# Neighbourhood attention in tiles of 64 queries of two heads by 128 keys, on one Trainium2 core

## What is computed

```python
col_start = np.clip(c - WIN_COLS // 2, 0, GRID_W - WIN_COLS)
col_mask = (c[None, :] >= col_start[:, None]) & (c[None, :] < col_start[:, None] + WIN_COLS)
s = jnp.einsum("brwhd,brkvhd->bhrwkv", qg, k_rows,
               preferred_element_type=jnp.float32) * (NA_HEAD_DIM ** -0.5)
s = jnp.where(col_mask[:, None, :], s + bias, NEG_INF)
p = jax.nn.softmax(s.reshape(B, NA_HEADS, rows, GRID_W, kr * GRID_W), axis=-1)
o = jnp.einsum("bhrwkv,brkvhd->brwhd", p, v_rows)
```

## Time and profile before

| | us |
|---|---|
| median of three runs | 2140.15 |
| lowest, highest | 2139.81, 2140.32 |
| span of the profiled execution | 2138.8 |
| TensorE busy in it | 2126.1 (99%) |
| VectorE busy | 1417.7 (66%) |
| ScalarE busy | 1094.5 (51%) |

### The profile page before, as it was taken

One profiled execution on the slowest core, in us unless ns is written; L12 is line 12 of the kernel. 1 busy time (PEld: TensorE's weight loads), 2 busy tenths in 40 slices (PEclk: granted clock), 3 DMA queues, 4 the chain that ended last, 5 costly groups with the idle time before them and its releaser, 6 DMA issues.

```text
span 2138.8 us, 27241 instructions
## 1 busy us (share of the span) xinstructions
PE 2126.1 (99%) x9684; PEld 1758.9 (82%) x9684; DVE 1417.7 (66%) x1952; ACT 1094.5 (51%) x1515; POOL 59.7 (3%) x70
## 2 busy tenths in 40 slices
PE   9999999999999999999999999999999999999999
PEld 7888887888888888888877888888888888888887
DVE  6998767765655656656667645766445876766764
ACT  6545565654444444444566544555444665565452
POOL 1000100000000000000000000000000010000000
PEclk9999999999999999999999999999999999999999
DMA  9555446676766766767566765666666775666985
GB/s 329 187 187 163 154 150 211 208 217 197 239 201 207 212 203 205 208 195 217 169 209 200 242 190 167 205 195 202 206 198 196 227 208 175 188 186 193 343 263 165
DMA packets 198773, 439.43 MB, mean 205 GB/s; under 512 B 93928, under 2 KB 94576, under 8 KB 198384
## 3 DMA queue, kind: packets, MB, share of 16 engines
q1 hardware_dynamic: 196608, 431.79, 65.3%
q0 software_dynamic: 1744, 5.77, 0.9%
q10 hardware_dynamic: 288, 0.14, 0.0%
HBM read 407.73 MB, written 10.49 MB: 196 GB/s over the span
## 4 chain that ended last, share of the span: by engine, by line
PE 93%; DVE 3%; ACT 1%; DMA 1%; issue 1%; SPq 1%; POOL 0%; ACTq 0%; DVEq 0%
PE g L644 29%; PE g L646 29%; PE g L645 29%; DVE wlo L1502 1%; DMA raw<-in_w_in 1%; PE s L623 1%; DVE arena L1872 1%; PE s L701 1%; SPq L2415 1%; PE s L832 0%; PE s L831 0%; ACT whi L921 0%; PE s L683 0%; DVE ta_lo L1688 0%; PE s L693 0%
## 5 line engine op out<-in xcount | busy, mean ns | idle before, releaser
L1502 DVE TENSOR_TENSOR wlo<-raw,whi 128x1024 fp32r<-128x1024 f32 x732 | 888.6, 1222 | 524.0 <-ACT whi L921 522.3
L921 ACT ACTIVATE whi<-raw 128x1024 fp32r<-128x1024 f32 x732 | 768.9, 1057 | 671.5 <-PE g L646 600.8
L644 PE MATMUL g<-whi,ta_hi 128*128 128x512 f32 x1920 | 760.0, 396 | 6.6 <-DVE wlo L1502 1.7
L646 PE MATMUL g<-whi,ta_lo 128*128 128x512 f32 x1920 | 748.7, 390 | 0.0
L645 PE MATMUL g<-wlo,ta_hi 128*128 128x512 f32 x1920 | 747.6, 389 | 0.0
L644 PEld LDWEIGHTS g<-whi,ta_hi 128*128 128x128 f32 x1920 | 360.7, 188 | 84.3 <-issue 8.1
L646 PEld LDWEIGHTS g<-whi,ta_lo 128*128 128x128 f32 x1920 | 360.5, 188 | 76.3
L645 PEld LDWEIGHTS g<-wlo,ta_hi 128*128 128x128 f32 x1920 | 361.0, 188 | 72.6
L644 PE MATMUL g<-whi,tb_hi 128*128 128x512 f32 x1008 | 396.7, 394 | 0.2 <-ACT arena L1110 0.2
L646 PE MATMUL g<-whi,tb_lo 128*128 128x512 f32 x1008 | 392.8, 390 | 0.0
L645 PE MATMUL g<-wlo,tb_hi 128*128 128x512 f32 x1008 | 392.5, 389 | 0.0
(11 more groups left out here) (239 smaller groups left out, 996.5 us busy)
## 6 DMA issues: line engine op xcount, KB each, us to landing
raw<-in_w_in SPq DMA_DIRECT2D x318, 512.0 KB, 3.9
raw<-in_w_up SPq DMA_DIRECT2D x128, 512.0 KB, 4.2
raw<-in_w_down SPq DMA_DIRECT2D x128, 512.0 KB, 4.2
raw<-in_w_out SPq DMA_DIRECT2D x64, 512.0 KB, 4.4
raw<-in_w_a SPq DMA_DIRECT2D x32, 512.0 KB, 4.1
raw<-in_w_b SPq DMA_DIRECT2D x32, 512.0 KB, 6.3
raw<-in_w_ukv SPq DMA_DIRECT2D x16, 512.0 KB, 4.0
raw<-in_w_uq SPq DMA_DIRECT2D x12, 512.0 KB, 3.8
```

Of the source, the lines that this page charges most:

```text
L644: e.matmul(o, xh, wh, start=first, stop=False)
L646: ins = e.matmul(o, xl, wh, start=False, stop=last)
L921: e.activation(whi[u % RING][:, 0:n], raw[u % RAW][:, 0:n], ACT.Copy).then_inc(s_hi, 1)
L1502: e.tensor_tensor(l, r, h.bitcast(F32), ALU.subtract).then_inc(s_lo, 1)
```

## The change

A tile is now 64 queries (16 columns) of both heads of a pair by 128 keys (32 columns); windows of keys begin at 0, 32, 96, 128. A pair has four such tiles, side by side in one bank, and is handled as a whole (8 instead of 16 rounds). GpSimd arranges Q instead of K (`na_qm`). VectorE adds the bias for all pairs and, after the exponential, multiplies the weights by the reciprocal; then they are turned. In the output product V stands (is loaded) and the turned weights pass, so that the output arrives turned and `ya_side` goes away. A window of V that isn't one of V's own halves is copied by SyncE into the stage buffer (`window_side`). The starts are slots 109, 121, 133, 145, 151, 170, 179, 188; scaling three slots later, turns six, output nine.

```diff
-        NA0 = [E("v0") - 4 + 6 * i for i in range(8)] + [E("v1") + (-4, 0, 12, 16, 20, 24, 28, 32)[i] for i in range(8)]
-        YA0 = [NA0[7] + 8, NA0[15] + 8]
-
+        NA0 = [E("v0") - 2 + 12 * i for i in range(4)] + [E("v1") + i for i in (-8, 11, 20, 29)]
+        NA_N, NA_T, NA_O = 4, 6, 9
...
+        def value_window(pr, t):
+            a, b = pr * P, (pr % 4) * P
+            return V1[:, t // 2, a:a + P] if t in (0, 3) else SG[2 + pr // 4][:, t - 1, b:b + P]
```

TensorE:

```diff
-                        b = bank(0, (na_e, i + 1) if pr < 4 else (na_m, i + 1))
-                        q.wait_ge(qk_c, 4 * (pr // 4) + (pr % 4) // 2 + 1)
-                        q.wait_ge(km_f, 2 * pr + 2)
-                        km = na_km[pr % 2].rearrange("p (h n) -> p h n", h=2)[:, :, KEY0[it]:KEY0[it] + KEYS]
-                        ins = e.matmul(two_heads(b), QT1[:, pr, it * P:(it + 1) * P], km, start=True, stop=pr >= 4)
-                        if pr < 4:
-                            q.wait_ge(d_bias[i % 4], 16 * (i // 4 + 1))
-                            ins = e.matmul(two_heads(b), ident, na_p[i % 4], start=False, stop=True)
+                        b = bank(0, (na_m, pr + 1))
+                        q.wait_ge(qk_c, 4 * n + 2 + (pr % 4) // 2 + 1)
+                        q.wait_ge(qm_f, 2 * pr + 2)
+                        for t in range(4):
+                            ins = e.matmul(b[:, t * P:(t + 1) * P], na_qm[pr % 2][:, t * P:(t + 1) * P],
+                                           KT1[:, pr, WINDOW[t]:WINDOW[t] + P], start=True, stop=True)
...
-                        q.wait_ge(na_e, i + 1)
-                        for c in range(4):
-                            ins = e.transpose(b[:, c * P:(c + 1) * P], na_w[i % 4][:, c * P:(c + 1) * P], ident)
+                        q.wait_ge(na_n, pr + 1)
+                        for t in range(4):
+                            ins = e.transpose(b[:, t * P:(t + 1) * P], p[:, t * P:(t + 1) * P], ident)
...
-                        for h in range(2):
-                            for jt in range(2):
-                                ins = e.matmul(b[:, h * 64:(h + 1) * 64],
-                                               na_tb[i % 2][:, h * 256 + jt * P:h * 256 + (jt + 1) * P],
-                                               V1[:, jt, pr * P + 64 * h:pr * P + 64 * h + 64], start=jt == 0, stop=jt == 1)
+                        b = bank(1, (ya_h, pr + 1), (ya_l, pr + 1))
+                        q.wait_ge(na_tc, pr + 1)
+                        q.wait_ge(v_e, n + 1)
+                        q.wait_ge(d_vw[n], 64)
+                        for t in range(4):
+                            ins = e.matmul(b[:, t * P:(t + 1) * P], value_window(pr, t), tb[:, t * P:(t + 1) * P],
+                                           start=True, stop=True)
```

ScalarE:

```diff
+                    if part == "e":
+                        q.wait_ge(na_m, pr + 1)
+                        for t in range(4):
+                            ins = e.activation(p[:, t * P:(t + 1) * P], p[:, t * P:(t + 1) * P], ACT.Exp,
+                                               bias=na_mx[k][:, t:t + 1], accum_out=na_sm[k][:, t:t + 1])
...
+                        q.wait_ge(na_o, pr + 1)
                         for h in range(2):
+                            ins = e.activation(rows_of(tb_hi[:, 8 + pr, :], 64 * h), heads_of(sps[1][:, :], h, 64 * h), ACT.Copy)
+                        ins.then_inc(ya_h, 1)
```

VectorE:

```diff
+                        q.wait_ge(na_s, pr + 1)
+                        q.wait_ge(d_bias[k], 16 * (pr // 4 + 1))
                         if pr >= 4:
+                            q.wait_ge(na_e, pr - 3)
+                        q.wait_ge(dve_own, own.then(e.tensor_tensor(na_p[k], sps[0][:, :], na_p[k], ALU.add)))
+                        e.tensor_reduce(na_mx[k], tiles, AX.X, ALU.max, negate=True).then_inc(na_m, 1)
+                    elif part == "r":
+                        q.wait_ge(na_e, pr + 1)
+                        q.wait_ge(dve_own, own.then(e.reciprocal(na_rc[k], na_sm[k])))
+                        e.tensor_tensor(tiles, tiles, na_rc[k].unsqueeze(2).to_broadcast([P, 4, P]), ALU.mult).then_inc(na_n, 1)
```

SyncE, new:

```diff
+            def window_side():
+
+                for n in range(2):
+                    yield E(f"v{n}") + 2
+                    q.wait_ge(v_e, n + 1)
+                    q.wait_ge(*((u_d, 2), (u_t, 4))[n])
+                    v, w = V1[:, :, n * 512:(n + 1) * 512], SG[2 + n]
+                    e.dma_start(w[0:96, 0], v[32:128, 0]).then_inc(d_vw[n], 16)
+                    e.dma_start(w[96:128, 0], v[0:32, 1]).then_inc(d_vw[n], 16)
+                    e.dma_start(w[0:32, 1], v[96:128, 0]).then_inc(d_vw[n], 16)
+                    e.dma_start(w[32:128, 1], v[0:96, 1]).then_inc(d_vw[n], 16)
```

More of the change, by code:

```diff
@@ L382, in two_blocks @@
         ln6, lnmv = [stat(12), stat(12)], [stat(2), stat(2)]
-        na_mx, na_sm, na_rc = ([stat(2) for _ in range(4)] for _ in range(3))
+        na_mx, na_sm, na_rc = ([stat(4) for _ in range(4)] for _ in range(3))
         uN, eN, kss = stat(16), stat(16), stat(2)
@@ L397, in two_blocks @@
         d_bias = [sem(f"d_bias{i}") for i in range(4)]
+        d_vw = [sem(f"d_vw{i}") for i in range(2)]
         d_ys = [sem(f"d_ys{i}") for i in range(4)]
@@ L578, in na_parts @@
         def na_parts():
[L580 to L581 removed]
+            t = [(NA0[i], "s", i) for i in range(8)] + [(NA0[i] + NA_T, "t", i) for i in range(8)]
+            return sorted(t + [(NA0[i] + NA_O, "o", i) for i in range(8)])
         def at_parts():
@@ L992, in na_side @@
             def na_side():
-                parts = [(NA0[i], "e", i) for i in range(16)] + [(NA0[i] + 4, "c", i) for i in range(16)]
-                for slot, part, i in sorted(parts + [(NA0[i] + 6, "x", i) for i in range(16)]):
+                parts = [(NA0[i], "e", i) for i in range(8)] + [(NA0[i] + NA_T, "tc", i) for i in range(8)]
+                for slot, part, pr in sorted(parts + [(NA0[i] + NA_O, "y", i) for i in range(8)]):
                     yield slot
-                    pr, it, k = i // 2, i % 2, i % 4
+                    n, k = pr // 4, pr % 4
+                    p = na_p[k]
@@ L1580, in na_side @@
             def na_side():
-                parts = [(NA0[i], "m", i) for i in range(16)] + [(NA0[i], "r", i) for i in range(16)]
-                for slot, part, i in sorted(parts):
+                parts = [(NA0[i], "m", i) for i in range(8)] + [(NA0[i] + NA_N - 1, "r", i) for i in range(8)]
+                for slot, part, pr in sorted(parts + [(NA0[i] + NA_O, "y", i) for i in range(8)]):
                     yield slot
-                    pr, k = i // 2, i % 4
+                    k = pr % 4
+                    tiles = na_p[k].rearrange("p (t n) -> p t n", t=4)
@@ L1594, in na_side @@
-                        e.tensor_reduce(na_mx[k], src, AX.X, ALU.max, negate=True).then_inc(na_m, 1)
-                    else:
-                        q.wait_ge(na_e, i + 1)
-                        if i >= 4:
-                            q.wait_ge(na_x, i - 3)
-                        e.reciprocal(na_rc[k], na_sm[k]).then_inc(na_r, 1)
-            def ya_side():
-                for n in range(2):
-                    for pair in range(2):
-                        yield YA0[n] + 2 * pair
-                        k = 2 * n + pair
-                        q.wait_ge(ya_h, k + 1)
-                        kt = 8 + 2 * k
-                        e.tensor_tensor(in_rows(tb_lo[:, kt:kt + 2, :]), in_columns(two(TBK["ya", k])),
-                                        in_rows(tb_hi[:, kt:kt + 2, :].bitcast(F32)), ALU.subtract).then_inc(ya_l, 1)
+                            q.wait_ge(na_e, pr - 3)
```

192 lines of the change are left out of this document (78 added, 114 removed).

## The result

The changed kernel takes **2149.03 us** (median of four runs, 2147.92 to 2151.39), the kernel before beside it 2140.24 (2139.81 to 2140.99): a ratio of 1.0042, 95% interval 1.0027 to 1.0056. It is slower by 8.8 us, where the likeliest case said 3 us and reached to 2147 by its bounds; the nearest of the cases is that of the late copies, 2148. The profiled execution is the lowest of the four, 2147.92, with a span of 2146.0.

The account below looks back on a forecast made before the run. TensorE's own work set the pace, with VectorE next and without reserve during the convolution. Terms: -20.2 + 8.4 + 7.0 + 1.8 + 0.9 + 2.7 + 1.8 + 0.8 = +3.2 us on 2140.15, so 2143; range 2132 to 2150.

Parts of the forecast that it names:

- the likeliest case: The forecast itself: whole kernel at 2143 us, between 2139 and 2147 by its bounds; chance 0.55.
- the late copies: Rival: copies of V take over 3.5 us from issue; with 7.1, +5 us, 2148; chance 0.15.
- TensorE's saving: Attention stage: removed work 36.4 us, added 18.2, saved 18.2; with 2 of old waits 20.2 us.
- VectorE's pace: First half, to v1: a pair takes VectorE 21.0 us, TensorE 18.6; TensorE waits 8.4 us in all.
- output of pair 0, for its copies: Copies of v0's windows land about when this output is due; wait 0.
- output of pair 4, for its copies: Slot 160, after v1: TensorE waits 7 us for SyncE's copies of V, issued by 5.0, landing 3.5 later.
- lower clock behind it: After the idle stretch of 7 us TensorE falls to 1.2 GHz: 1.8 us, bounds 0 and 3.5.
- bank of mixp2: At mixc0, TensorE waits 2.7 us for ScalarE's copy of mixp2, which comes behind four exponentials.
- turns of pairs 5 and 6: After slot 161, scaling of pair 5 keeps its turns 1.8 us, that of pair 6 0.8.
- the rival with TensorE's count alone: All waits small, so only TensorE's own work counts: 2122 to 2128 us; chance 0.10.
- The rival in which VectorE isn't the bound: Only the last of each wait remains, 1 of the 8.4 us: 2136; chance 0.13.
- the stand: VectorE stands 1.85 us per pair while ScalarE takes four exponentials before the weights' high half of the same slot.

Follow-up runs that it names:

- the last kernel: Changed kernel with exponentials one slot later, output of pair 4 eight, pairs 5 to 7 two, pair 5's turns and pair 0's output two, pair 5's output one: 2122.31 us.
- experiment 4: Changed kernel without the copies of V; the middle tiles' output products read V's own halves, so middle windows get wrong keys: 2138.68 us.
- experiment 5: Changed kernel with SyncE taking the copies of V two slots sooner, at the slot of v0's and v1's end: 2148.65 us.
- experiment 1: Changed kernel with the four exponentials of each pair one slot later in ScalarE's list, behind the high half of the scores' slot: 2138.47 us.
- experiment 2: Changed kernel without VectorE's scaling of the weights; reciprocals still computed, attention output left unnormalised: 2145.78 us.
- experiment 6: Changed kernel with the third and fourth copy of V issued by GpSimd instead of SyncE: 2149.21 us.
- experiment 7: Changed kernel with the output of pair 4 eight slots later on all engines, slot 168 instead of 160: 2138.29 us.

## Why the prediction was nearly right

The mechanism was right in its main parts: TensorE's saving, VectorE as the bound up to v1, one long wait for the copies. Several sizes were not, and two costs stood at nothing. Term by term, in us:

| term | forecast | measured | by what |
|---|---|---|---|
| TensorE's own work and its old waits | -20.2 | about -20 | the last kernel: -18.2 with 2.3 of waits left |
| VectorE's pace (turns of pairs 0 to 4, output of 3) | 8.4 | 8.0 | 0.9, 1.3, 2.0, 1.2, 0; 2.6 |
| lower clock behind the output of pair 3 | 0 | 1.6 | window at 243.3 |
| output of pair 0, for its copies | 0 | 1.7 | list of waits |
| output of pair 4, for its copies | 7.0 | 9.5 | list of waits |
| lower clock behind it | 1.8 | 1.5 | window at 264.1 |
| second LayerNorm turns | 0.9 | 0.9 | |
| bank of mixp2 | 2.7 | 2.8 | |
| turns of pairs 5 and 6 | 1.8, 0.8 | 1.6, 0.2 | |
| sum | +3.2 | about +8 | stage: +7.8 |

(The waits of the column "measured" are from the end of the stream's last product to the first product of the group, up to 0.2 more than the profile's idle times.)

- **TensorE's saving** was right. That the rival with TensorE's count alone (2122 to 2128) was wrong for this kernel and right for the last one, 2122.3, is the best support of the sum: the 18 to 20 us are in the tiles, and the order of other engines' work had spent them.
- **VectorE's pace** was right in its cause. The rival in which VectorE isn't the bound falls. That the sum came out near 8.4 is partly luck: the single waits are off by up to 1.1 us both ways. The pace itself was too fast, 21.0 us a pair for 21.6 to 21.7: in the first two periods addition, maximum and stand took 3.4 and 3.5 us for 3.2, the low halves of an output 1.2 and 0.9 for 0.75. The missing time stands in the next row but one of the table. With VectorE as the bound, the wait at pair 0's output is no cost of its own: experiments 4 and 5 take it away, and the first stretch gets longer. One point was coarse: the stand was one summand of 21.0 us a pair, beside the work. Experiments 1 and 2 part them: in the first stretch the order is worth 10.8 us (94.86 to 84.09), the scaling 1.8, and some 3 if the copies of v0 had not held up the first period (an estimate, four periods at 0.75).
- **The term that was mis-sized is the value copies.** "One load and four copies at 0.33 for an issue; the last is issued at 5.0 and lands 3.5 later." The copies took 0.54 to 0.59 us each in SyncE's queue, so the last was issued at 6.0, and it landed 4.7 later: 2.5 us more at pair 4. The same two numbers gave the output of pair 0 a wait of 1.7 where I had put 0 with "both some 10 us after v0". That is the milder form of the rival "the copies land late": its condition, over 3.5 us from issue, came true with 3.8 to 4.7, inside my bounds of 2.8 to 7.1. The mistake was in the choice of row: a weight load of one block was taken for a copy of part of the partitions to others. By the Trainium skill ("DMA: Bandwidth & Descriptors", section "Anatomy of one DMA") the last copy would have taken some 2.4 us, an estimate from its fixed part and its bytes. The figures of the Trainium skill there are fitted on DMAs that GpSimd issues, and SyncE issued this one; the run shows 4.7, and the measurement decides.
- **The clock.** I charged the fall behind the long wait, and it cost what I charged. I did not ask whether a shorter wait would do: the one of 2.4 us at the output of pair 3 did, for 1.6 us.
- **Not in the stage**: some 1.0 us. The spans of the two profiled executions differ by 7.2 us, the medians of the runs by 8.8. In the record an execution's time is 1.8 to 2.0 us above its span, so the span of 2138.8 belongs to an execution of some 2140.6, 0.4 above its median; the changed kernel's profiled execution is the lowest of its four, 1.1 below their median. What differs between its executions wasn't traced. The clock stayed up behind mixp2 in the profiled one and fell there in eight profiles of experiments with a wait of 2.6 to 2.9 us at that point or just behind it. That can be a part of it and not all: the execution of 2148.69 us has a mean granted clock of 0.997, the profiled one, 0.8 us shorter, 0.996.

Nearly all that was missed lies on one side: 2.5 us at pair 4, 1.7 at pair 0 (in truth VectorE's pace), 1.6 of clock. So the time came out above the bounds of the likeliest case, and the range held it only because of the late copies, a case with a chance of 0.15. Together these terms decide between "no change" and "slower by 0.4%": a sum of +20 and -20 is known no better than its parts.

## What to carry to other kernels

When a change makes the bounding engine's work shorter, the saving is real only where the others' fixed order is due sooner too. Go through every list of slots again, ask for each engine what stands ahead of the piece that the next one waits for, and move the piece that nobody needs soon (here exponentials whose sums VectorE takes up three slots later, ahead of a high half that it needs in the same slot). And when a wait is removed, look at the next meeting point with the second engine before claiming its length: in experiments 4 to 6 the wait at pair 0's output came back at the turns of pair 1. In experiment 7 the removed wait did not come back, and the second engine had reserve there: in the changed kernel VectorE is busy for 20.4 of the 39.1 us between v1 and slot 175.

## What the runs showed of the hardware

- **Short waits can cost the clock.** TensorE was at 1.2 GHz behind waits of 2.4 us (output of pair 3, also in experiments 2 and 4 to 7), 2.9 to 3.0 us (turns of pair 1, experiments 4 to 6) and 2.6 to 2.9 us (mixp2 or pair 5's turns, in the experiments). Not behind each: the wait of 2.7 us for mixp2 left it at 2.4 GHz in the changed kernel, and in experiment 1 brought it down for 6.8 us. The wait of 1.8 us at the turns of pair 2 did not do it. Where it fell, an estimated 1 to 3 us were lost beside the wait (half of TensorE's busy time in the stretch). In the last kernel, with no wait over 1 us, it did not fall at all.
- **A copy within SBUF is not a load.** Copies of 64 and 192 KB between partitions took 0.54 to 0.65 us each to issue on SyncE, where a weight load takes 0.33, 0.51 to 0.53 on GpSimd, and landed 3.8 to 4.7 us after issue, up to 5.6 when two queues issued them at a time. The 64 KB copies were no faster than those of 192 KB (4.0 to 4.4 and 3.8 to 4.7 in the changed kernel); of the four each next one took longer to land, 3.8 to 4.1 us for the first and 4.6 to 4.7 for the last, both of 192 KB.
